# Ranking the expert groups by size and running the smallest group's experts in pairs, in plain fp32 on column strips

## The chip, the cores and the metric

The kernel runs on 1 core of one Trainium2 chip. The metric is the device time of one execution in microseconds (us). TensorE is called PE here (PEld is its weight load), VectorE is DVE, ScalarE is ACT, GpSimd is POOL and SyncE, which issues nearly all DMAs of this kernel, is SP.

## The reference, cut to what matters

Two transformer blocks are computed for 256 tokens of width 1024. The change touches only the last stage, a mixture of 16 experts in four groups of four:

```python
p_group = jax.nn.softmax((t @ w_rg + b_rg).astype(jnp.float32), axis=-1)
g_val, g_idx = lax.top_k(p_group, 1)                 # one group for each token
fine_sel = jnp.take_along_axis(fine, g_idx[:, :, None], axis=1)[:, 0]
e_val, e_idx = lax.top_k(jax.nn.softmax(fine_sel, axis=-1), TOP_K_IN_GROUP)
...
for e in range(N_EXPERTS):
    y_e = (jax.nn.silu(t @ w1[e]) * (t @ w3[e])) @ w2[e]     # 1024x512, 1024x512, 512x1024
    out = out + combine[:, e:e + 1] * y_e
```

Each token belongs to one group, so the four groups' token counts add up to 256, and the smallest group has at most 64 tokens. All weights are fp32: 6 MB for an expert, 96 MB for the stage.

## The kernel before, in words

**Weights.** Every weight is brought by SP in units of 512 KB (128 partitions x 1024 values). A unit lands in a landing buffer (L365, `load_unit`). ACT copies it rounded into a ring of 8 buffers (`weights_hi`, L396, `split_hi`), and DVE subtracts that from the landed unit into a second ring (`weights_lo`, L408, `split_lo`). PE multiplies with both parts in three matmuls (high x high, high x low, low x high: `three`, L443). In the expert stage there are 8 landing buffers (`expert_stage`: four `stage`, two in `x_and_ctx`, two in `work`). SP loads unit u only after `split_lo` of unit u-8 (`lo_ready`), and SP's program is in order: one load that waits holds all behind it. The ring is given back by `unit_used`, which PE raises after a unit's last matmul.

**Experts.** The router's results decide the tokens. The group in the first place is computed densely for all 256 tokens (weights stationary, 8 units "up" for w1 and w3, 4 units "down" for w2). The other three groups have their tokens gathered by selection matrices (`SEL`, 128 slots for each group, matmul L1912) and are computed with the gathered tokens stationary and the weights moving, 512 columns at a time. After four experts of such a group the summed result is split in two parts (`block_hi`, `block_lo`) and scattered back to the tokens by matmuls (`scatter`, L2020). The sequence is written by hand in `SEQ`: dense, four slot experts, dense, four, dense, four, dense.

**Order on the engines.** Step p of the loop does on PE: up with w1, the transposes of the hidden rows of step p-1 (`expert_turn`, L1972), up with w3, and down of step p-1. The units are loaded in the same order: up of p (w1, then w3), then down of p-1. DVE does in step p: the splits of down of p-1 and of up of p+1, with the product of step p (`expert_product`, L3287 and L3294) ahead of the last four splits, and the parts of a scatter in between. ACT does the silu of step p, the hidden rows of p-1 and the 12 splits.

**Set-up.** Between the router and the first expert DVE works out which groups have over 128 tokens, a running sum of those, and from it the slots (L3199 to L3233) and the four first experts for SP (`expert_order`). Then come 8 gathers of 384 columns on PE, each read by two ACT and two DVE instructions (L2449, L2450, L3267, L3270), and the slot weights (L1928).

## Time and profile before

| | us |
|---|---|
| median of 3 runs | 1610.04 |
| lowest, highest | 1608.06, 1612.14 |
| profiled execution: span from the first to the last instruction | 1604.0 |
| what a timed run has beside the span (median less span) | 6.0 |
| PE busy in the span | 1547.5 (96%) |
| expert stage, from PE's first expert matmul at 1257.49 to its last at 1600.04 | 342.6 |

The page gives each engine's busy time. Its strips cut the span into 40 equal slices with a digit each. In the expert stage, the last nine slices, PE stands at 9 throughout, and the DMA strip is at 7 to 9 until the last slice but one. The granted clock is 1.00 in the whole expert stage.

### The profile page before, as it was taken

Reading aid. Unit: us, or ns where it says so; the run is one execution under the profiler, and the core shown is the slowest. Engines: PE = TensorE matmul, PEld = TensorE weight load, DVE = VectorE, ACT = ScalarE, POOL = GpSimd, SP = SyncE. Lnnn points to the kernel's source line nnn. Section 1 sums busy time; section 2 is a strip of 40 time slices with the busy share of each in tenths; the row PEclk is TensorE's granted clock in tenths of the full one; section 3 lists DMA queues with packets and bytes.
Section 4 is the critical chain, followed back from the end, with each engine's and each line's share of the span. In section 5 each row is a group of like instructions: output and inputs, shape, how many; then the busy total and the mean of one; then the engine's idle time right before and its main releaser. Section 6 shows DMA issues by size and latency. Waiting matters only on the chain.

```text
span 1604.0 us, 24065 instructions
## 1 busy us (share of the span) xinstructions
PE 1547.5 (96%) x8757; PEld 1261.9 (79%) x8757; DVE 1090.1 (68%) x1726; ACT 838.2 (52%) x1342; POOL 14.0 (1%) x36
## 2 busy tenths in 40 slices
PE   6999999999999999999999999998998999999999
PEld 3865558988888889888659999886776888889888
DVE  3447764854444446878977676887775687786894
ACT  4326554722322325688864544654453566666672
POOL 2000000000000000000010000000000000000000
PEclk9999999999999999999999999999999999999999
DMA  9588633422332332434525665543220789788792
GB/s 350 162 346 312 247 122 103 153 71 92 103 93 93 103 99 59 122 90 131 173 64 171 192 187 186 171 152 96 93 92 1 263 298 380 247 329 311 256 380 81
DMA packets 195799, 279.69 MB, mean 174 GB/s; under 512 B 12434, under 2 KB 111220, under 8 KB 190588
## 3 DMA queue, kind: packets, MB, share of 16 engines
q1 hardware_dynamic: 194308, 274.21, 50.6%
q0 software_dynamic: 1152, 4.19, 0.7%
q8 instruction: 56, 0.92, 0.2%
q14 instruction: 35, 0.29, 0.1%
q10 hardware_dynamic: 248, 0.09, 0.0%
HBM read 277.40 MB, written 1.05 MB: 174 GB/s over the span
## 4 chain that ended last, share of the span: by engine, by line
PE 76%; DVE 10%; ACT 7%; DMA 3%; issue 2%; SPq 0%; POOL 0%; DVEq 0%; ACTq 0%; POOLq 0%
PE bank L443 66%; DVE weights_lo L408 2%; PE bank L1540 2%; DMA ada_rows_in<-in_ada_w_dram 2%; PE bank L745 1%; ACT weights_hi L396 1%; PE bank L1381 1%; PE bank L1365 1%; DVE work L2781 1%; DVE softmax_cols L2648 1%; PE bank L1349 1%; ACT work L2118 1%; DVE x_and_ctx L590 1%; DMA stage<-in_lru_w_i_dram 1%; DVE work L2639 1%
## 5 line engine op out<-in xcount | busy, mean ns | idle before, releaser
L408 DVE TENSOR_TENSOR weights_lo<-stage,weights_hi 128x1024 fp32r<-128x1024 f32 x324 | 385.1, 1220 | 48.4 <-ACT weights_hi L396 44.6
L396 ACT ACTIVATE weights_hi<-stage 128x1024 fp32r<-128x1024 f32 x324 | 330.1, 1056 | 114.3 <-PE bank L443 69.4
L443 PE MATMUL bank<-act_hi,weights_hi 128*128 128x256 f32 (+1 forms) x1040 | 324.6, 312 | 1.3 <-DVE act_lo L553 1.0
L443 PE MATMUL bank<-act_lo,weights_hi 128*128 128x256 f32 (+1 forms) x1040 | 323.1, 311 | 0.0
L443 PE MATMUL bank<-act_hi,weights_lo 128*128 128x256 f32 (+1 forms) x1040 | 323.1, 311 | 0.0
L443 PE MATMUL bank<-weights_hi,ff_hi 128*128 128x512 f32 x568 | 221.6, 390 | 0.2 <-DVE ff_lo L3031 0.2
L443 PE MATMUL bank<-weights_hi,ff_lo 128*128 128x512 f32 x568 | 221.1, 389 | 0.0
L443 PE MATMUL bank<-weights_lo,ff_hi 128*128 128x512 f32 x568 | 221.0, 389 | 0.0
L443 PEld LDWEIGHTS bank<-act_hi,weights_hi 128*128 128x128 f32 x1040 | 198.3, 191 | 14.5 <-DVE act_lo L553 1.5
L443 PEld LDWEIGHTS bank<-act_lo,weights_hi 128*128 128x128 f32 x1040 | 198.3, 191 | 11.2
L443 PEld LDWEIGHTS bank<-act_hi,weights_lo 128*128 128x128 f32 x1040 | 198.3, 191 | 10.5
L443 PE MATMUL bank<-weights_hi,act_hi 128*128 128x512 f32 (+1 forms) x448 | 177.4, 396 | 6.2 <-ACT work L2315 1.8
L443 PE MATMUL bank<-weights_lo,act_hi 128*128 128x512 f32 (+1 forms) x448 | 173.8, 388 | 0.0
L443 PE MATMUL bank<-weights_hi,act_lo 128*128 128x512 f32 (+1 forms) x448 | 173.5, 387 | 0.0
L845 ACT ACTIVATE turn<-bank 128x512 f32<-128x512 f32 (+1 forms) x48 | 23.6, 492 | 205.6 <-PE bank L443 205.6
L443 PEld LDWEIGHTS bank<-weights_hi,ff_hi 128*128 128x128 f32 x568 | 106.7, 188 | 22.2 <-DVE ff_lo L3031 0.3
L443 PEld LDWEIGHTS bank<-weights_lo,ff_hi 128*128 128x128 f32 x568 | 106.6, 188 | 22.2
L443 PEld LDWEIGHTS bank<-weights_hi,ff_lo 128*128 128x128 f32 x568 | 106.7, 188 | 21.5
L443 PEld LDWEIGHTS bank<-weights_hi,act_hi 128*128 128x128 f32 x448 | 84.6, 189 | 27.8 <-issue 9.2
L867 DVE TENSOR_TENSOR work<-work,bank 128x512 f32<-128x512 f32 x72 | 49.4, 686 | 79.5 <-PE bank L443 79.5
L443 PEld LDWEIGHTS bank<-weights_lo,act_hi 128*128 128x128 f32 x448 | 84.5, 189 | 17.5
L443 PEld LDWEIGHTS bank<-weights_hi,act_lo 128*128 128x128 f32 x448 | 84.6, 189 | 15.6
(404 smaller groups left out, 2018.5 us busy)
## 6 DMA issues: line engine op xcount, KB each, us to landing
stage<-in_mlp_w_dram SPq DMA_DIRECT2D x128, 512.0 KB, 4.0
stage<-in_w_dram SPq DMA_DIRECT2D x96, 512.0 KB, 6.1
ada_rows_in<-in_ada_w_dram SPq DMA_DIRECT2D x40, 1024.0 KB, 6.5
x_and_ctx<-in_w_dram SPq DMA_DIRECT2D x48, 512.0 KB, 5.9
work<-in_w_dram SPq DMA_DIRECT2D x48, 512.0 KB, 6.2
stage<-in_w_in_dram SPq DMA_DIRECT2D x32, 512.0 KB, 4.2
stage<-in_lru_w_in_dram SPq DMA_DIRECT2D x20, 512.0 KB, 3.9
stage<-in_attn_w_qkv_dram SPq DMA_DIRECT2D x12, 512.0 KB, 7.9
```

The source lines that it names most:

```text
L396: act.eng.activation(whi[u % NRING][:], landing(act, u)[:], ACT.Copy).then_inc(sem("hi_ready"), 1)
L408: dve.eng.tensor_tensor(wlo[u % NRING][:], landing(dve, u)[:], whi[u % NRING][:].bitcast(F32), ALU.subtract).then_inc(sem("lo_ready"), 1)
L443: m = pe.eng.matmul(ps, l, r, start=start and j == 0, stop=stop and j == 2, skip_group_check=True)
L590: dve.eng.scalar_tensor_tensor(out=XC[:, tt, :], in0=T, scalar=cc[:, 12 + tt:13 + tt], in1=XC[:, tt, :], op0=ALU.mult, op1=ALU.add).then_i ...
L745: m = pe.eng.matmul(psum[bank][32 * q:32 * q + 32, :], adastat[:, k, :], ada_in[ada_buf(p)][:, q * 512:q * 512 + 512], start=k == 0, stop= ...
L845: act.eng.activation(tbuf[:, m % 2, 0:T], ps[:, 0:T], ACT.Relu).then_inc(*act.free((tag, "h", m)))
L867: dve.eng.tensor_tensor(dst, dst, ps[:], ALU.add).then_inc(*dve.free(key))
L1349: m = t.matmul(ps[:], q, kT[rows, j, :], start=False, stop=True, skip_group_check=True)
L1365: m = t.transpose(ps[:, c0:c0 + P], prob[h % 3][:, i, n * P:(n + 1) * P], ident[:])
L1381: m = t.matmul(ps[64 * a:64 * a + 64, i * P:(i + 1) * P], V[:, kt, 2 * j + i, :], pT[:, n, a, i * P:(i + 1) * P], start=n == 0, stop=n == ...
L1540: t.matmul(psum[2 * n + tt][:], SUM[:, 2 * kp + kk, tt * P:(tt + 1) * P], out_rows(kp, n)[:, kk, :], start=kp + kk == 0, stop=False, skip_ ...
L2118: s.activation(prob[h % 3][:, i, 0:nk], ps[:, 0:nk], ACT.Exp, bias=sm[:, 0, at + i:at + i + 1], scale=HD ** -0.5, accum_out=sm[:, 1, at + ...
```

## The change

Four things change, all in the expert stage and its set-up.

1. DVE ranks the four groups by token count with MAX and MAX_INDEX. The largest group is the dense one, the next two have 128 slots each, and the smallest has 64 slots, held twice side by side. The gather has 320 columns, and of the smallest group only a plain fp32 copy is kept (`GP`).
2. The smallest group's four experts run as two pair steps, one behind the other, between the second and the third dense expert. In a pair step one expert's matmul writes PSUM partitions 0 to 63 and the other's 64 to 127, with 64 stationary columns each (two column strips of the array). Operands are plain fp32, and the moving operand is the landed unit itself: no `split_hi`, no `split_lo`.
3. The units of a pair are not split, so their landing buffers are given back by PE (`unit_used`) instead of by DVE (`lo_ready`).
4. The pair results are added up in a buffer (`YP`) by ACT and DVE (`pair_y`, `pair_add`), split (`pair_hi`, `pair_lo`) and scattered in step 9. The last block of slot experts is scattered in the last down step, as the third block was before.

Steps are numbered by their place in `STEPS` from here on. The units that a text numbers count from the first unit of the expert stage (unit 0) in load order; there are 192 before and after.

```diff
@@ sequence of steps @@
-        SEQ = [0, 4, 5, 6, 7, 1, 8, 9, 10, 11, 2, 12, 13, 14, 15, 3]
+        STEPS = [("dense", 0), ("slots", 4), ("slots", 5), ("slots", 6), ("slots", 7), ("dense", 1), ("pair", 12),
+                 ("pair", 14), ("dense", 2), ("slots", 8), ("slots", 9), ("slots", 10), ("slots", 11), ("dense", 3)]
+        SCATTER_STEP = {6: 0, 9: 2}
@@ load_unit (SP) @@
-                if before >= 0:
-                    sp.eng.wait_ge(sem("lo_ready"), before + 1)
+                if before >= 0 and whole(before):
+                    sp.eng.wait_ge(sem(USED), before + 1)
+                elif before >= 0:
+                    sp.eng.wait_ge(sem("lo_ready"), split_index(before) + 1)
...
@@ expert_up (PE), pair step @@
+                if kind(p) == "pair":
+                    for kq in range(4):
+                        w = pair_begin(pe, (2, 512))
+                        for kk in range(2):
+                            k = 2 * kq + kk
+                            for e in range(2):
+                                mm = t.matmul(ps[HD * e:HD * e + HD, :], GP[:, k, 0:HD], w[e][:, kk, :], start=k == 0,
+                                              stop=k == KT - 1, skip_group_check=True)
+                                if kk:
+                                    mm.then_inc(sem(USED), 1)
...
@@ expert_down (PE), pair step @@
+                    for f in range(4):
+                        w = pair_begin(pe, (1, 1024))
+                        for n in range(2):
+                            for m in range(2):
+                                mm = t.matmul(psum[6 + n][HD * m:HD * m + HD, :],
+                                              HP[:, f, HD * m:HD * m + HD],
+                                              w[m][:, 0, n * 512:n * 512 + 512], start=f == 0, stop=f == 3,
+                                              skip_group_check=True)
+                                if n:
+                                    mm.then_inc(sem(USED), 1)
...
@@ scatter (PE) @@
-                t.wait_ge(*pe.freed(("y", b, n)))
+                t.wait_ge(*pe.freed(("y", b, n)) if b < 2 else pe.at("pair_lo", n + 1))
...
@@ pair results (ACT) @@
+            def pair_y(p):
+                for n in range(2):
+                    at = slice(n * 512, n * 512 + 512)
+                    if p == EXPERT_PAIRS[0]:
+                        s.wait_ge(*act.filled(("yp", p, n)))
+                        s.activation(YP[:, at], plan.bank(("yp", p, n))[:], ACT.Copy).then_inc(*act.free(("yp", p, n)))
+                    else:
+                        s.wait_ge(*act.freed(("yp", p, n)))
+                        s.wait_ge(*act.filled(("sc", 0, n, 1)))
+                        s.activation(Yhl[:, 0, at], YP[:, at], ACT.Copy).then_inc(*act.mark("pair_hi"))
...
@@ loop over the steps (DVE) @@
+            for p in range(LAST + 1):
                 if ends_block(p - 2):
                     block_lo(block_of(p - 2))
+                if p - 2 == EXPERT_PAIRS[1]:
+                    pair_add(p - 2)
...
+                todo = split_count(p - 1, "down") + split_count(p + 1, "up")
                 if p:
                     expert_hidden_lo(p - 1)
-                    split_lo(dve, 2)
-                if ends_block(p - 2):
-                    block_sum(block_of(p - 2), 0)
-                split_lo(dve, 6 if p else 4)
+                    todo = some_lo(todo, 2)
+                if p - 2 == EXPERT_PAIRS[1]:
+                    pair_lo()
+                if p in SCATTER_STEP:
+                    block_sum(SCATTER_STEP[p], 0)
+                todo = some_lo(todo, 6 if p else 4)
                 expert_product(p)
...
+                todo = some_lo(todo, 4)
@@ gather (ACT and DVE), 8 times @@
-                s.activation(G3H[:, d, :], ps[:, TX:384], ACT.Copy, scale=colA[:, d, 0:1]).then_inc(*act.mark("g_hi"))
+                s.activation(GP[:, d, 0:HD], ps[:, TX:320], ACT.Copy, scale=colA[:, d, 0:1]).then_inc(*act.mark("g_hi"))
-                v.scalar_tensor_tensor(out=G3L[:, d, :], in0=ps[:, TX:384], scalar=colA[:, d, 0:1],
-                                       in1=G3H[:, d, :].bitcast(F32), op0=ALU.mult,
-                                       op1=ALU.subtract).then_inc(*dve.free(("gather", d)))
```

**On DVE, from the product that ends the dense or pair work to the scatter's second part.** Before, in the step behind a block of slot experts (the second such place), DVE's rows read as follows; L3287 is the dense product, L3326 the second part of the block's result, L3303 the hidden rows, L408 the split.

```order
L3287 TENSOR_TENSOR work<-work,bank 128x512 [waits bank2_full,bank0_free]
L3287 TENSOR_TENSOR work<-work,bank 128x512 [waits unit_used,bank1_free]
L408 TENSOR_TENSOR weights_lo<-x_and_ctx,weights_hi 128x1024 [waits hi_ready,unit_used] x2
L408 TENSOR_TENSOR weights_lo<-work,weights_hi 128x1024 [waits hi_ready,unit_used] x2
L3326 TENSOR_TENSOR y_hi_lo<-bank,y_hi_lo 128x512 [waits y_hi] x2
L3303 TENSOR_TENSOR ff_lo<-work,ff_hi 128x2x256 [waits e_hi] x2
L408 TENSOR_TENSOR weights_lo<-stage,weights_hi 128x1024 [waits hi_ready,unit_used] x2
L3334 TENSOR_TENSOR x_and_ctx<-x_and_ctx,bank 128x512 [waits bank4_full]
L3334 TENSOR_TENSOR x_and_ctx<-x_and_ctx,bank 128x512 [waits bank5_full]
```

The block's second part (L3326) stands ahead of the splits, and the four splits ahead of it belong to units loaded long before. Now the rows of steps 8 and 9 read so; L447 is the split, L3395 the product of the second pair, L3388 the dense product, L3437 the addition of the pair results, L3444 the second part for the scatter.

```order
L3395 SCALAR_TENSOR_TENSOR turn<-turn,decay_coefs,bank 128x512 [waits unit_used,bank0_free]
L447 TENSOR_TENSOR weights_lo<-stage,weights_hi 128x1024 [waits hi_ready,unit_used] x4
L447 TENSOR_TENSOR weights_lo<-x_and_ctx,weights_hi 128x1024 [waits hi_ready,unit_used] x2
L447 TENSOR_TENSOR weights_lo<-work,weights_hi 128x1024 [waits hi_ready,unit_used] x2
L3388 TENSOR_TENSOR work<-work,bank 128x512 [waits bank2_full,bank0_free]
L3388 TENSOR_TENSOR work<-work,bank 128x512 [waits unit_used,bank1_free]
L3437 TENSOR_TENSOR work<-work,bank 128x512 [waits bank6_free,unit_used]
L3437 TENSOR_TENSOR work<-work,bank 128x512 [waits bank7_free,unit_used]
L3404 TENSOR_TENSOR ff_lo<-work,ff_hi 128x2x256 [waits e_hi] x2
L447 TENSOR_TENSOR weights_lo<-stage,weights_hi 128x1024 [waits hi_ready,unit_used] x2
L3444 TENSOR_TENSOR y_hi_lo<-work,y_hi_lo 128x512 [waits pair_hi] x2
```

All eight splits of the next slot expert's up units (L447, x4, x2, x2) now stand between the second pair's product and the dense product, and two more splits stand ahead of the scatter's second part.

**On SP, the loads of the next slot expert's first units.** Before, at the same kind of place:

```order
L365 ISA [waits lo_ready]
L365 DMA stage<-in_w_2_dram 128x2x512
L365 ISA [waits lo_ready]
L365 DMA stage<-in_w_2_dram 128x2x512
L365 ISA [waits lo_ready]
L365 DMA stage<-in_w_2_dram 128x2x512
L365 ISA [waits lo_ready]
L365 DMA stage<-in_w_2_dram 128x2x512
L365 DMA x_and_ctx<-in_w_2_dram 128x2x512 [waits lo_ready] x2
L365 DMA work<-in_w_2_dram 128x2x512 [waits lo_ready] x2
```

Now, behind the loads of the second pair's w2 (128x1024 rows, for which `lo_ready` is awaited):

```order
L400 ISA [waits unit_used]
L400 DMA stage<-in_w_2_dram 128x2x512
L400 ISA [waits unit_used]
L400 DMA stage<-in_w_2_dram 128x2x512
L400 ISA [waits unit_used]
L400 DMA stage<-in_w_2_dram 128x2x512
L400 ISA [waits unit_used]
L400 DMA stage<-in_w_2_dram 128x2x512
L400 DMA x_and_ctx<-in_w_2_dram 128x2x512 [waits unit_used] x2
L400 DMA work<-in_w_2_dram 128x2x512 [waits unit_used] x2
L400 DMA stage<-in_w_2_dram 128x1024 [waits lo_ready] x4
```

The eight loads of step 9's up units wait for `unit_used`, that is for PE's down step of the second pair, where they waited for a split before.

## Rows read from the trace of the kernel before

**Rows 1.** The page: span, busy time (x instructions), and the DMA strip.
```profile
span 1604.0 us, 24065 instructions
PE 1547.5 (96%) x8757; PEld 1261.9 (79%) x8757; DVE 1090.1 (68%) x1726; ACT 838.2 (52%) x1342; POOL 14.0 (1%) x36
...
DMA  9588633422332332434525665543220789788792
```
**Rows 2.** Busy time by stretch: us, PE, PEld, DVE, ACT, POOL, clock, DMA share, GB/s.
```profile
1345.00:1395.00 50.00, 50.00 (x315) 45.42 (x314) 36.33 (x38) 31.76 (x37) 0.00 (x0) 1.00 0.78 279
```
**Rows 3.** Waits of SP's queue from 1240 to 1604: total us, times, longest.
```profile
SPq L365 <- DVE weights_lo L408: 225.0, 183, 9.1
```
**Rows 4.** PE in order of time: start us, us, engine, line, one slot expert apart.
```profile
1307.84 0.38 PE L1972 MATMUL bank<-ident,turn 128*128 128x128 f32 x2
...
1324.65 0.38 PE L1972 MATMUL bank<-ident,turn 128*128 128x128 f32 x2
```
**Rows 5.** Plain fp32 products: 32- and 64-column strips in time order, full width by group.
```profile
103.52 0.13 PEld L745 LDWEIGHTS bank<-ada_rows_in,ada_stat 128*32 128x32 f32 x4 [0.30 <-issue]
103.95 0.13 PEld L745 LDWEIGHTS bank<-ada_rows_in,ada_stat 128*32 128x32 f32 x4 [0.30 <-issue]
...
124.16 1.97 PE L1381 MATMUL bank<-work 128*64 128x128 f32 x32
...
L1540 PE MATMUL bank<-ada_rows_in,work 128*128 128x512 f32 x64 | 27.7, 593 | 1.2 <-ACT turn L2239 1.2
```
**Rows 6.** Busy time by stretch, columns as in Rows 2, two with DMA full.
```profile
1320.00:1325.00 5.00, 5.00 (x26) 4.13 (x25) 4.55 (x5) 1.57 (x3) 0.00 (x0) 1.00 1.04 420
...
1530.00:1535.00 5.00, 5.00 (x25) 4.14 (x24) 3.21 (x4) 4.27 (x6) 0.00 (x0) 1.00 1.04 394
```
**Rows 7.** DMA issues from 1367.5, behind a pause: the first alone, then four; median us to landing.
```profile
stage<-in_w_dram SPq DMA_DIRECT2D x1, 512.0 KB, 3.6
...
stage<-in_w_dram SPq DMA_DIRECT2D x4, 512.0 KB, 5.1
```
**Rows 8.** ACT in order of time while it waits for landings.
```profile
1336.00 1.06 ACT L396 ACTIVATE weights_hi<-stage 128x1024 fp32r<-128x1024 f32 x1 [0.26 <-DMA stage<-in_w_dram]
1337.31 1.06 ACT L396 ACTIVATE weights_hi<-stage 128x1024 fp32r<-128x1024 f32 x1 [0.25 <-DMA stage<-in_w_dram]
```
**Rows 9.** Groups by line from 1300 to 1600: busy us, mean ns of one.
```profile
L408 DVE TENSOR_TENSOR weights_lo<-stage,weights_hi 128x1024 fp32r<-128x1024 f32 x83 | 96.5, 1219 | 7.6 <-ACT weights_hi L396 7.5
L3303 DVE TENSOR_TENSOR ff_lo<-work,ff_hi 128x512 fp32r<-128x512 f32 x6 | 3.9, 689 | 5.7 <-ACT ff_hi L2480 5.6
L3287 DVE TENSOR_TENSOR work<-work,bank 128x512 f32<-128x512 f32 x6 | 3.8, 680 | 0.0
L396 ACT ACTIVATE weights_hi<-stage 128x1024 fp32r<-128x1024 f32 x82 | 82.3, 1057 | 18.5 <-PE bank L443 14.6 <-DMA stage<-in_w_dram 3.9
L2480 ACT ACTIVATE ff_hi<-work 128x512 fp32r<-128x512 f32 x6 | 3.5, 626 | 2.0 <-DVE work L3287 2.0
```
**Rows 10.** Set-up: DVE in order of time, gather parts by group, PE in order of time.
```profile
1242.45 0.15 DVE L3199 TENSOR_SCALAR work<-bank 128x4 f32<-128x4 f32 x1
...
1245.04 0.75 DVE L3233 TENSOR_SCALAR select<-slot_numbers,work 128x384 fp32r<-128x384 f32 x2
...
L3270 DVE SCALAR_TENSOR_TENSOR gathered_lo<-bank,col_scale,gathered_hi 128x128 fp32r<-128x128 f32 x6 | 2.1, 343 | 0.0
...
1256.16 1.47 PE L1928 MATMUL bank<-work,select 128*128 128x4 f32 x12 [0.20 <-DVE gathered_lo L3270]
1257.49 0.36 PE L443 MATMUL bank<-act_hi,weights_hi 128*128 128x256 f32 x1
```
**Rows 11.** PE behind a pause, and the clock by stretch (columns as in Rows 2).
```profile
1098.52 0.47 PE L443 MATMUL bank<-weights_hi,act_hi 128*128 128x512 f32 x1 [1.83 <-ACT work L2315]
...
1105.68 0.49 PE L1768 MATMUL bank<-ident,work 128*128 128x128 f32 x3
...
1100.00:1102.00 2.00, 2.00 (x6) 1.53 (x5) 1.86 (x5) 0.00 (x0) 0.00 (x0) 0.50 0.83 248
```

More of the change, by code:

```diff
@@ L437, in unit_end, with pair_begin @@
                 plan.entry[key]["full"] = pe.last
+        def pair_begin(pe, shape):
+            views = []
+            for _ in range(2):
+                u = pe.unit
+                pe.eng.wait_ge(*pe.at(*landed(pe, u)))
+                views.append(landing(pe, u)[:].rearrange("p (a b) -> p a b", a=shape[0]))
+                pe.unit += 1
+            return views
         def three(pe, ps, wh, wl, ah, al, start, stop, stationary_weights):
@@ L1953, in expert_up @@
                 ps = pe.take(("h", p, j), 2 * j)
+                if kind(p) == "pair":
[8 more added lines that the diff above has]
+                                    mm.then_inc(sem(USED), 1)
+                    pe.last = (USED, Affine(pe.unit, 0, 1))
+                    plan.entry[("h", p, j)]["full"] = pe.last
+                    return
                 gh, gl, at = slots(block_of(p))
-                if SEQ[p] == 4 and j == 0:
+                if expert(p) == 4 and j == 0:
                     for d in range(KT):
@@ L1976, in expert_down @@
                 c0 = TX * (p % 2)
-                e = SEQ[p]
+                e = expert(p)
+                if kind(p) == "pair":
+                    t.wait_ge(*pe.freed(("T", p)))
+                    for n in range(2):
+                        t.wait_ge(*pe.bank_free(6 + n))
+                        pe.take(("yp", p, n), 6 + n)
+                    for f in range(4):
[8 more added lines that the diff above has]
+                                    mm.then_inc(sem(USED), 1)
+                    pe.last = (USED, Affine(pe.unit, 0, 1))
+                    for n in range(2):
+                        plan.entry[("yp", p, n)]["full"] = pe.last
+                    return
                 for f in range(4):
@@ L2485, in expert_hidden_hi @@
                 ps = plan.bank(("T", p))
+                if kind(p) == "pair":
+                    s.activation(HP, ps[:].rearrange("p (f t) -> p f t", f=4),
+                                 ACT.Copy).then_inc(*act.free(("T", p)))
+                    return
                 s.activation(fhi[:, :, c0:c0 + P], ps[:].rearrange("p (f t) -> p f t", f=4),
@@ L3214, in _ @@
-            for r in range(3):
-                v.tensor_scalar(idx[:, 1 + r:2 + r], upto[:, r:r + 1], 4.0, 4.0 * r, ALU.mult, ALU.add).then_inc(*dve.mark())
-            v.wait_ge(*dve.own())
-            v.tensor_copy(order[:], idx).then_inc(*dve.mark("expert_order"))
-            base = rt(14, 4)
-            v.scalar_tensor_tensor(out=base, in0=wide, scalar=128.0 - 1048576.0, in1=first_slot[:, 0, :], op0=ALU.mult,
+            ranked, slot, one = rt(9, 8), rt(11, 2, 4), rt(13, 4)
+            wide, ahead = rt(10, 4), rt(14, 4, 4)
@@ L3221, in _ @@
+            rank = rt(15, 4)
+            v.wait_ge(sem("slots"), 3)
+            v.scalar_tensor_tensor(out=group_keys[:, 0:4], in0=ps[:, 8:12], scalar=8.0, in1=prio[:], op0=ALU.mult,
                                    op1=ALU.add).then_inc(*dve.mark())
             v.wait_ge(*dve.own())
-            v.scalar_tensor_tensor(out=base, in0=upto, scalar=-128.0, in1=base, op0=ALU.mult, op1=ALU.add).then_inc(*dve.mark())
+            v.max(out=ranked, in_=group_keys[:]).then_inc(*dve.mark())
             v.wait_ge(*dve.own())
-            v.tensor_tensor(slot, ps[:, 0:8].rearrange("p (t g) -> p t g", t=2),
-                            base.unsqueeze(1).to_broadcast([P, 2, 4]), ALU.add).then_inc(*dve.free("count"))
+            v.max_index(out=order[:], in_max=ranked, in_values=group_keys[:]).then_inc(*dve.mark("group_order"))
@@ new lines, in _ @@
+            v.tensor_tensor(ahead, ranked[:, 0:4].unsqueeze(1).to_broadcast([P, 4, 4]),
+                            group_keys[:, 0:4].unsqueeze(2).to_broadcast([P, 4, 4]), ALU.is_gt).then_inc(*dve.mark())
+            v.wait_ge(*dve.own())
+            v.tensor_reduce(rank, ahead, AX.X, ALU.add).then_inc(*dve.mark())
+            v.wait_ge(*dve.own())
+            v.scalar_tensor_tensor(out=slot, in0=rank.unsqueeze(1).to_broadcast([P, 2, 4]), scalar=512.0,
+                                   in1=ps[:, 0:8].rearrange("p (t g) -> p t g", t=2), op0=ALU.mult,
+                                   op1=ALU.add).then_inc(*dve.free("count"))
@@ L3305, in expert_hidden_lo @@
                     return
+                if kind(p) == "pair":
+                    return
                 v.wait_ge(sem("e_hi"), hidden_count(p))
```

219 lines of the change are left out of this document (128 added, 91 removed).

## The prediction, made before the changed kernel was run

> **What bounds the kernel now.** I read the page first: PE is busy for 96% of the span, and the DMA strip stands at 7 to 9 in the expert stage [rows 1]. Then the stage by stretches: in 50 us around two steps PE is busy for all 50 at full clock, and DMA for 0.78 of it [rows 2]. So PE sets the end, with DMA close behind it. The waits of SP's queue come third: loads waited 225 us in all for DVE's splits, 183 times [rows 3]. Landing buffers are full and the stream is held back by consumers, never the other way round. From this the question is what a faster PE finds when it asks for units sooner than now.
>
> **PE work.** Two transposes of the same kind stand one slot expert apart, 16.81 us [rows 4]; four such experts are 67.2. A pair step has 2 x 8 contraction steps up and 4 x 2 down, 24 in all, each of two plain fp32 matmuls of 512 columns, one on each strip. The plain 128x512 product takes 27.7 us for 64 records, 0.43 each, and a plain matmul is two records (L1540 issues 32), so 0.86 [rows 5]. Do two strips share that time? L745's four strips do: each quarter has one record in every 0.43 us. L1381 has strips of 64 columns, in pairs as here: 32 records of 128 columns in 1.97 us, one pair in 0.113 after the last one's 0.27, where 128 columns alone need a quarter of 0.43, that is 0.107 [rows 5]. So a pair step is 24 x 0.86 = 20.6 us, with 0.45 of transposes 21.1, and two are 42.2. PE work falls by 67.2 - 42.2 = 25.0 us. From the other side, strips that don't overlap would make it 83.5 instead, 16 more than now; I take the overlap, which two rows show.
>
> The Trainium skill (TensorE: Matmul & The Clock Gate, "Measured speedup vs the span model") measured 2.38 times for three column strips, a share of 0.79 each. By that rule the two steps' matmuls would be 41.2 / 0.79 = 52 us and the saving 11 less. The rows with four strips at one strip's pace speak against it.
>
> **Set-up.** From the count to the selection DVE does 13 dependent small steps in 2.59 us, 0.2 each [rows 10]; now there are 8, two of them (MAX, MAX_INDEX) not in this trace. At 0.2 each this is 1.0 us sooner; between 0.15 and 0.5 for those two it is 0.4 to 1.1. Then each gather loses DVE's second part, 0.34 long, and the slot weights wait for the fifth gather's DVE part (PE sat idle for it) [rows 10]: five times 0.34 is 1.7, less the overlap of one instruction with the next; I take 1.3. The first expert starts right behind, so 2.3 us sooner; 1 to 3.
>
> **DMA in the pair steps.** With the DMA full, 394 to 420 GB/s were moved [rows 6]; 0.524 MB is 1.25 to 1.33 us a unit, and ACT, waiting for landings, began one each 1.31 [rows 8]. I take 1.32. Behind a pause the first unit landed 3.6 us after its issue, and four issued one behind another had a median of 5.1 [rows 7], where a steady 1.32 would give 3.9; I put the fourth at 9.6 after the first issue. A pair step asks for a unit each 0.86 us, and its whole units sit in the landing buffers till PE has used them.
>
> Count from PE's start of the first pair with eight units landed. Two units are used each 1.72, so the first load goes out at 1.8, the ninth unit lands at 5.4, the twelfth at 11.4, the sixteenth at 16.7, and up ends at 18.4 instead of 14.7 (with the scatter, 0.9). Next come the four w2 units of the dense step: they land at 18 to 22, need ACT 1.06 and DVE 1.22 [rows 9], and the down step needs two of them, since the first block sum, which frees its banks, stands behind two splits on DVE. It starts near 22 and lasts 10.9. In it PE frees no pair unit: eight units of the second pair land by 32.5, then the queue runs dry until 34.8. The next lands at 38.5, the fourth at 44, and the 16 behind it at 1.32 each, the last of the first pair's w2 at 60; the third dense expert's first unit lands at 61.5 and is split at 63.8. PE's own work up to there is 13.8 + 0.9 x 2 + 10.9 + 13.8 + 0.45 + 6.9 = 47.7. Lost: 16 us. If the queue never ran dry and the restarts cost nothing, 37 units by 1.3 still give 56, so 8 is the least; with a landing rate as slow as 1.45 it is 20.
>
> The Trainium skill (DMA: Bandwidth & Descriptors, "Specifications") gives a core about 358 GB/s of HBM. A unit would then be 1.46 us, and this loss near 20. The trace of this core alone shows 394 to 420.
>
> **The step behind the pairs.** The dense expert is 23 us of PE, in which the second pair's eight w2 units land and fill all buffers. The next loads wait for `unit_used` of the down step. Count from its start: first load at 1.8, first landing 5.4, fourth 11.4, eighth 16.7. Down ends at 6.9; the up step's fourth unit is ready at 11.4 + 2.4 = 13.8, so up with w1 ends at 15.1 instead of 12.3: 2.8 lost. Then comes the scatter, and what it waits for stands on DVE behind all of this: eight splits (the last ends at 19.1), the dense product, two parts of 0.68 that overlap a little (20.4), the pair sums, two parts again (21.7), on ACT the second high part (22.2), the silu (22.8) and the hidden rows (23.8), again on DVE their low part (24.5), two splits (26.8), and the first low part of the pairs (27.5) [rows 9]. PE stands from 15.1 to 27.5. Lost in all: 15.2 us; 11 if the splits come as fast as the buffers allow and ACT runs ahead, 18 with landings as late as the worst.
>
> Behind such a pause the clock matters. Behind a wait of 1.83 us on ACT the granted clock was 0.50 for a stretch of 2 us, that is 1.2 of 2.4 GHz, and the 24 matmuls up to the next transposes took 7.2 us. At 0.227 each, (16.81 - 0.45) / 72 of a slot expert [rows 4], they would take 5.4 [rows 11]. I add 1.6 for the one long pause, between 0 and 3.4.
>
> **What costs nothing.** 48 splits fewer on ACT and as many fewer on DVE (1.06 and 1.22 us each [rows 9]) free engines that wait for PE anyway. The pair sums of the first pair (ACT, 2 x 0.6) are under the dense up. The tail is the same as before: scatter, last down, four sums, stores.
>
> **Sum against the profiled execution.** -25.0 - 2.3 + 16 + 15.2 + 1.6 = +5.5. Span 1604.0 + 5.5 = 1609.5; the median has 6.0 more than the span, so 1615.5. Most of PE's saving goes to the two waits.
>
> **The rivals.** What a measurement of this kernel can tell from no change is about 0.3%, or 4.8 us: 1605.2 to 1614.9.
> - No change that can be told: the same mechanisms at the small end, 10 us in the pair steps and 12 behind them: -25 - 2.3 + 10 + 12 + 1 = -4 up to +4.8. For it: both ends above are reachable from rows. Time near 1611. Chance 0.31.
> - Faster: the supply isn't the limit, since PE's stream of whole units and less traffic by ACT and DVE let DMA keep up, and the scatter's operand is ready sooner. 8 in the pairs and 3 behind them: -16, 1594. For it: in the dense steps DMA had pauses to spare (0.78 busy). Against it: no landing can be ahead of a buffer that isn't free, and the DVE order is in the program. Chance 0.12.
> - Slower by strips that don't overlap: from the point where a pair's two matmuls take over 1.3 us, PE rather than the DMA sets the pace. Pairs 83.5, so +16 for PE, no wait in the pairs, 10 behind them, -2.3: +24, 1634. Against it: rows 5. Chance 0.04.
> - Slower by supply: landings at 1.46, or a clock that stays at the lower level while PE waits a third of each step (then a step is 3.4 us and PE-bound): +5 to +10 on the forecast, 1622. Chance 0.06.
> - The forecast, over 1614.9: 0.47.
>
> So slower by over 0.3% has 0.57, no change 0.31, faster 0.12. For eight in ten I leave out the lowest tenth and the upper: 1605 to 1624.
>
> **What would show it.** Right: PE in the two pair steps idle with DMA named as what ended it, DMA share near 1.0 there; one wait of 10 to 14 us at the scatter matmul in step 9, ended by DVE (L3444); PE's busy time about 25 lower; records of the pair matmuls in twos, 0.43 apart; the first expert matmul near 1255. Wrong in the first place: no wait at that scatter, or pair steps of 21 us without waits (then it is faster), or records of the two strips one behind the other (then it is far slower).

## The result, and the profile after

| | before | after |
|---|---|---|
| median of the first comparison, us | 1609.05 (4 runs) | 1625.78 (4 runs) |
| ratio, 95% interval | | 1.0101 (1.0083 to 1.012) |
| median of a second comparison, us | 1609.87 (23 runs) | 1622.91 (6 runs) |
| ratio, 95% interval | | 1.0066 (1.004 to 1.0093) |
| profiled execution, span | 1604.0 | 1621.5 (its own time 1623.24) |

One of the four runs of after (1923.9 at 0.75 of the clock) counts in the median but not in the ratio; without it the median is 1624.75. The change makes the kernel slower, by 0.7 to 1.0%, where 0.3% was forecast (1615.5, with 1605 to 1624 as the range).

The page of after, against [rows 1]: span, PE's busy time, and the strips of the clock and of DMA.

```profile
span 1621.5 us, 23657 instructions
PE 1536.1 (95%) x8653; PEld 1227.2 (76%) x8653; DVE 1032.2 (64%) x1662; ACT 791.2 (49%) x1292; POOL 14.0 (1%) x36
...
PEclk9999999999999999999999999999999999999899
DMA  9588733423233332334435566452221788787692
```

PE's busy time fell by 11.4 us, not by 25. Of the missing 13.6 us 10.5 are work at the lower clock (12.2 us lost in after and 1.7 in before, as counted below); the other 3.1 are not traced. Where the saving went is seen in the expert stage cut at PE's landmarks (columns as in [rows 2]): up to the first pair matmul, the first pair's up, the second dense down, the second pair's up, the first pair's down, the third dense up, the second pair's down, the next slot expert's w1, the wait at the scatter, and what follows.

```profile
1262.30:1386.60 124.30, 124.30 (x738) 110.68 (x737) 87.12 (x86) 72.50 (x82) 0.00 (x0) 1.00 0.81 292
1386.60:1407.30 20.70, 17.10 (x73) 5.76 (x72) 3.35 (x5) 3.96 (x7) 0.00 (x0) 1.00 0.84 315
1407.30:1422.50 15.20, 12.68 (x48) 10.07 (x48) 8.95 (x12) 2.62 (x3) 0.00 (x0) 0.89 0.71 262
1422.50:1440.90 18.40, 15.47 (x69) 4.92 (x68) 1.04 (x2) 1.15 (x2) 0.00 (x0) 1.00 0.85 313
1440.90:1453.00 12.10, 7.75 (x32) 2.29 (x32) 1.23 (x1) 2.11 (x2) 0.00 (x0) 1.00 1.04 397
1453.00:1476.60 23.60, 23.54 (x196) 23.52 (x196) 9.24 (x8) 9.02 (x11) 0.00 (x0) 1.00 0.69 265
1476.60:1485.30 8.70, 7.18 (x34) 2.21 (x32) 1.22 (x1) 2.11 (x2) 0.00 (x0) 1.00 0.57 185
1485.30:1492.70 7.40, 5.93 (x24) 4.32 (x24) 4.90 (x4) 4.23 (x4) 0.00 (x0) 1.00 1.04 396
1492.70:1505.10 12.40, 0.05 (x2) 0.00 (x1) 10.29 (x13) 8.66 (x12) 0.00 (x0) 0.65 0.85 321
1505.10:1514.80 9.70, 9.70 (x33) 7.78 (x34) 7.64 (x8) 3.90 (x4) 0.00 (x0) 0.74 0.71 237
```

Before, every such row reads PE busy for the whole stretch at 1.00. After, the rows without a wait in them are the first (124.3 of 124.3), the third dense up (23.5 of 23.6) and the last (9.7 of 9.7); the 103 us from there to the end have none either. In the rows of the pairs' up PE is idle for 3.6, 2.9 and 4.4 us while DMA moves 313 to 397 GB/s, and one row of 12.4 us has next to no PE at all. What ended PE's waits in the stage, the five largest (total us, times, longest):

```profile
PE bank L2121 <- DVE y_hi_lo L3444: 12.3, 1, 12.3
PE bank L495 <- DVE weights_lo L447: 7.5, 4, 2.5
PE bank L2029 <- DMA work<-in_w_dram: 2.8, 2, 2.1
PE bank L2029 <- DMA stage<-in_w_dram: 2.4, 4, 0.8
PE bank L2069 <- DMA stage<-in_w_dram: 1.9, 2, 1.3
```

And PE in order of time: the pair matmuls (16 records in 3.60 us, two strips in the time of one, as the strips of [rows 5]), a wait for a landing, the dense down, the scatter.

```profile
1390.16 3.60 PE L2029 MATMUL bank<-stage,work 128*64 128x512 f32 x16
...
1398.84 1.94 PE L2029 MATMUL bank<-work 128*64 128x512 f32 x8 [2.08 <-DMA work<-in_w_dram]
...
1409.83 0.47 PE L495 MATMUL bank<-weights_hi,ff_hi 128*128 128x512 f32 x1 [2.53 <-DVE weights_lo L447]
...
1505.10 2.08 PE L2121 MATMUL bank<-y_hi_lo,select_turned 128*128 128x512 f32 x4 [12.35 <-DVE y_hi_lo L3444]
```

For the dense down the profile names the split (L447). What came last there is the first block's sum (L3452), whose first half, 0.69 us long, ends 0.1 us ahead of PE's start at 1409.83:

```profile
1409.05 1.28 DVE L3452 TENSOR_TENSOR x_and_ctx<-x_and_ctx,bank 128x512 f32<-128x512 f32 x2
```

DVE during the long wait shows the order that the prediction read from the program: splits of the next slot expert, dense product (L3388), pair sums (L3437), hidden rows (L3404), two more splits, and at last the scatter's operand (L3444).

```profile
1493.96 2.50 DVE L447 TENSOR_TENSOR weights_lo<-work,weights_hi 128x1024 fp32r<-128x1024 f32 x2
1496.38 1.28 DVE L3388 TENSOR_TENSOR work<-work,bank 128x512 f32<-128x512 f32 x2
1497.57 1.27 DVE L3437 TENSOR_TENSOR work<-work,bank 128x512 f32<-128x512 f32 x2
1500.55 1.29 DVE L3404 TENSOR_TENSOR ff_lo<-work,ff_hi 128x512 fp32r<-128x512 f32 x2 [1.70 <-ACT ff_hi L2576]
1502.08 2.36 DVE L447 TENSOR_TENSOR weights_lo<-stage,weights_hi 128x1024 fp32r<-128x1024 f32 x2 [0.24 <-ACT weights_hi L432]
1504.36 1.28 DVE L3444 TENSOR_TENSOR y_hi_lo<-work,y_hi_lo 128x512 fp32r<-128x512 f32 x2
```

So far the forecast holds. But the first expert matmul is at 1262.34 and was at 1257.49, 4.9 us later instead of 2.3 sooner, though nothing ahead of the set-up was changed. Stretches of after at the granted clock of 0.50 to 0.54 explain it (columns as above):

```profile
124.00:127.00 3.00, 3.00 (x31) 2.98 (x32) 0.66 (x5) 1.54 (x5) 0.00 (x0) 0.54 1.03 429
1257.50:1260.90 3.40, 3.21 (x13) 3.17 (x14) 3.26 (x6) 3.40 (x10) 0.00 (x0) 0.50 1.05 398
1411.10:1414.50 3.40, 3.40 (x10) 2.63 (x9) 3.40 (x5) 0.00 (x0) 0.00 (x0) 0.50 1.05 384
1496.40:1505.10 8.70, 0.00 (x1) 0.00 (x1) 6.76 (x11) 6.53 (x9) 0.00 (x0) 0.50 0.78 285
1505.10:1510.00 4.90, 4.90 (x12) 3.84 (x13) 3.99 (x5) 0.23 (x1) 0.00 (x0) 0.50 0.56 190
```

The first of them stands in code that is the same in both kernels; in before it reads

```profile
124.00:127.00 3.00, 3.00 (x43) 2.72 (x42) 1.44 (x8) 1.79 (x6) 0.00 (x0) 1.00 1.03 429
```

with 12 matmuls more in the same 3 us. A stretch at 0.50 costs half of PE's busy time in it. Counted so over the whole trace, before lost 1.7 us to the clock, all at 1099.6, and after 12.2: 6.5 ahead of the set-up (of it 3.1 and 1.7 in two stretches at 1100 and 1134 that are not shown), 1.6 in it, 4.2 in the expert stage. So of the 17.5 us between the two spans 10.5 are the clock's.

### The profile page after: what moved, and what is told of

Read it like the earlier page. It is cut to its first block, busy times and chain, and to the rows that moved or that the text cites. A ratio compares the mean times of both kernels' runs of the same rounds, so it can differ in the third digit from the quotient of the medians.

```text
span 1621.5 us, 23657 instructions
## 1 busy us (share of the span) xinstructions
PE 1536.1 (95%) x8653; PEld 1227.2 (76%) x8653; DVE 1032.2 (64%) x1662; ACT 791.2 (49%) x1292; POOL 14.0 (1%) x36
## 4 chain that ended last, share of the span: by engine, by line
PE 70%; DVE 13%; ACT 7%; DMA 6%; issue 3%; SPq 1%; POOL 0%; DVEq 0%; ACTq 0%; POOLq 0%
PE bank L495 59%; DVE weights_lo L447 3%; DMA stage<-in_w_dram 2%; PE bank L1609 2%; ACT weights_hi L432 2%; DMA ada_rows_in<-in_ada_w_dram 2%; PE bank L797 1%; PE bank L1450 1%; PE bank L1434 1%; DVE work L2892 1%; PE bank L2029 1%; DVE x_and_ctx L2892 1%; DVE softmax_cols L2759 1%; PE bank L1418 1%; ACT work L2214 1%
## 5 line engine op out<-in xcount | busy, mean ns | idle before, releaser
L447 DVE TENSOR_TENSOR weights_lo<-stage,weights_hi 128x1024 fp32r<-128x1024 f32 x300 | 358.0, 1221 | 103.2 <-ACT weights_hi L432 96.7
L432 ACT ACTIVATE weights_hi<-stage 128x1024 fp32r<-128x1024 f32 x300 | 306.3, 1055 | 148.7 <-PE bank L495 67.7
L495 PE MATMUL bank<-weights_hi,ff_hi 128*128 128x512 f32 x536 | 210.6, 393 | 2.6 <-DVE weights_lo L447 2.5
L495 PE MATMUL bank<-weights_lo,ff_hi 128*128 128x512 f32 x536 | 209.8, 391 | 0.0
L495 PE MATMUL bank<-weights_hi,ff_lo 128*128 128x512 f32 x536 | 209.7, 391 | 0.0
L897 ACT ACTIVATE turn<-bank 128x512 f32<-128x512 f32 (+1 forms) x48 | 23.6, 491 | 206.4 <-PE bank L495 206.4
L495 PEld LDWEIGHTS bank<-weights_hi,ff_hi 128*128 128x128 f32 x536 | 101.4, 189 | 24.0 <-DVE weights_lo L447 2.9
L495 PEld LDWEIGHTS bank<-weights_lo,ff_hi 128*128 128x128 f32 x536 | 101.2, 189 | 21.4
L495 PEld LDWEIGHTS bank<-weights_hi,ff_lo 128*128 128x128 f32 x536 | 101.5, 189 | 20.5
L495 PEld LDWEIGHTS bank<-weights_hi,act_hi 128*128 128x128 f32 x448 | 85.4, 191 | 33.0 <-issue 12.3
```

Source lines behind the costliest of these rows:

```text
L432: act.eng.activation(whi[r % NRING][:], landing(act, u)[:], ACT.Copy).then_inc(sem("hi_ready"), 1)
L447: dve.eng.tensor_tensor(wlo[r % NRING][:], landing(dve, u)[:], whi[r % NRING][:].bitcast(F32), ALU.subtract).then_inc(sem("lo_ready"), 1)
L495: m = pe.eng.matmul(ps, l, r, start=start and j == 0, stop=stop and j == 2, skip_group_check=True)
L897: act.eng.activation(tbuf[:, m % 2, 0:T], ps[:, 0:T], ACT.Relu).then_inc(*act.free((tag, "h", m)))
```

## The experiments

For each profile three numbers serve below: the stage (first to last expert matmul), what the clock cost in it, counted as above, and the difference of the two. The timed runs were made in six comparisons, each with its own runs of before, whose median lay between 1608.6 and 1610.5; across comparisons the ratios to before are the safer measure. "Both" is the kernel with both reorderings of DVE that are described below, and "fillers" are matmuls that PE computes in its waits and nobody reads.

| kernel | median, us | ratio to before, 95% | stage | clock in stage | stage less clock |
|---|---|---|---|---|---|
| before (first profile) | | | 342.5 | 0 | 342.5 |
| before again | 1608.93 | 0.9993 (0.9979 to 1.0007) | 342.5 | 0 | 342.5 |
| after (first profile) | 1625.78 | 1.0101 (1.0083 to 1.012) | 355.1 | 4.2 | 350.9 |
| after again | 1622.91 | 1.0066 (1.004 to 1.0093) | 358.6 | 9.4 | 349.2 |
| sum first | 1622.57 | 1.007 (1.0048 to 1.0091) | 352.1 | 2.2 | 349.9 |
| pair results early | 1609.96 | 0.9995 (0.9978 to 1.0012) | 340.6 | 3.4 | 337.2 |
| both | 1606.58 | 0.9974 (0.9957 to 0.999) | 338.6 | 4.7 | 333.9 |
| quarter loads | 1611.47 (one run) | | 342.7 | 4.7 | 338.0 |
| pairs apart | 1609.89 | 0.9989 (0.997 to 1.0008) | 342.2 | 2.9 | 339.3 |
| down early | 1606.82 | 0.998 (0.9964 to 0.9995) | 338.2 | 0 | 338.2 |
| down early, fillers | 1603.68 | 0.996 (0.9947 to 0.9972) | 340.9 | 1.7 | 339.2 |
| after, fillers | 1614.34 | 1.0031 (1.002 to 1.0042) | 351.6 | 1.7 | 349.9 |
| both, fillers | 1602.10 | 0.9955 (0.9938 to 0.9972) | 335.5 | 0 | 335.5 |
| before, fillers | 1608.06 | 0.9987 (0.9973 to 1.0) | 342.5 | 0 | 342.5 |

**The two kernels again, unchanged.**

> The kernel before, unchanged. Its first profile shows one dip of the granted clock to 0.5 (3.4 us long, 1.7 us lost) in the whole span, the changed kernel's shows five ahead of the pair steps' own. Theory 'chance': the dips ahead of the expert stage come and go from one execution to the next in both kernels; then this profile has another number of them (2 to 5, span 1606 to 1611) at other places than 1100, and its timed runs spread in steps of about 1.7 us. Rival 'program': the kernel before has one dip ahead of the stage in each execution; then the profile again reads 1604 with a mean clock of 0.999.

> The changed kernel, unchanged. Theory 'chance': the dips at 124, 1134 and 1257 us of its first profile are not there again, or others are; PE's first expert matmul, 1262.3 in the first profile, moves by the dips' cost alone, 1.7 us each; the dips behind the waits of 2.5 and 12.3 us in the stage return or not, the waits themselves return within 0.5 us. Rival 'program': the same dips at the same places, first expert matmul again at 1262.3.

The profile of before now has a span of 1608.5. The stretch near 1100 is there again (at 1101.3, moved by the 1.7 us that one at 1077 cost), and two places are new, 1077 and 1193, where two are joined:

```profile
1077.40:1080.80 3.40, 3.40 (x8) 1.93 (x8) 3.30 (x6) 1.08 (x1) 0.00 (x0) 0.50 0.35 86
1101.30:1104.70 3.40, 3.40 (x10) 2.63 (x9) 3.19 (x7) 0.00 (x0) 0.00 (x0) 0.50 0.76 207
1193.40:1200.30 6.90, 5.95 (x14) 4.78 (x15) 3.95 (x6) 2.97 (x5) 0.00 (x0) 0.51 0.36 109
```

They cost 6.4 us, and its stage is 342.5 as before: the extra 4.5 us lie ahead of it. Over the 107 timed runs of before behind the first comparison the mean clock was 0.999 in three, and 0.992 to 0.998 in the others: the profile that I forecast from was one of the rare good ones. After again has its stretch at 124 no more, but others, among them 13.6 us around the start of the stage:

```profile
1256.20:1269.80 13.60, 12.40 (x57) 11.95 (x56) 12.17 (x17) 11.95 (x22) 0.00 (x0) 0.50 1.04 385
1501.90:1515.60 13.70, 6.10 (x14) 4.79 (x15) 10.21 (x14) 7.59 (x10) 0.00 (x0) 0.50 0.71 240
```

'Chance' is right for which stretches come ahead of the set-up, but not for where: every one of the 14 profiles has one near 1077 or near 1100, in before as in the changed kernels, and several places return. Nor is it the whole: one near 1257 (1251 to 1258) is there in all eight profiles of changed kernels without fillers (below), and in neither of the two of before; and one of 13.7 us, which starts inside the 12.3 us wait and goes on behind it, is there in all four profiles that have the wait unfilled. The wait itself came back at 12.3 both times. First expert matmul less the clock's cost ahead of it: 1255.8 and 1255.6 before, 1254.3 and 1254.0 after. The set-up is 1.6 us shorter.

Why the stretch near 1257 came with the change stays open. PE pauses there for 2.29 and 1.28 us in after, and the kernel before has nearly the same pauses at the same two gathers, with the clock at 1.00 in both of its profiles:

```profile
1250.98 0.44 PE L1912 MATMUL bank<-select,xn_hi 128*128 128x384 f32 x1 [2.10 <-DVE gathered_lo L3270]
...
1253.63 0.45 PE L1912 MATMUL bank<-select,xn_hi 128*128 128x384 f32 x1 [0.97 <-DVE gathered_lo L3270]
```

**Pair results early.** In DVE's loop (the dense product moves up together with the pair results and leaves its old place behind the splits; ACT takes the high part of the pair results behind the first two of its splits):

```diff
-                if p - 2 == EXPERT_PAIRS[1]:
-                    pair_add(p - 2)
...
+                if p - 1 == EXPERT_PAIRS[1]:
+                    expert_product(p)
+                    pair_add(p - 1)
                 if p:
                     expert_hidden_lo(p - 1)
                     todo = some_lo(todo, 2)
-                if p - 2 == EXPERT_PAIRS[1]:
+                if p - 1 == EXPERT_PAIRS[1]:
                     pair_lo()
...
-                expert_product(p)
+                if p - 1 != EXPERT_PAIRS[1]:
+                    expert_product(p)
```

> The changed kernel, where DVE takes in step 8 the dense product, the addition of the pair results and their low part ahead of the last six splits of the next slot expert, and ACT the high part behind the first two. Nothing else changes. Theory 'DVE's order' (my forecast's step behind the pairs): the wait of 12.3 us at the scatter goes, and with it the clock's 2.5 us; PE then waits for up w3's units only by their landings (1.3 us each against 1.36 that PE needs): 12 to 15 us faster than the changed kernel, about 1612. Rival 'supply': the units behind the restart at 1478 are late anyway, so the wait comes back in up w3 and in the dense down (whose hidden rows stand behind the splits on ACT): at most 6 us faster, about 1620.

13 us faster than after, in the same comparison: 'DVE's order'. The wait at the scatter is gone, and 12.0 of the 13 us are in the stage less clock. The pair sums (L3441) and their low part (L3448) now stand between splits that wait for landings anyway, five microseconds ahead of the scatter at 1493.60:

```profile
1483.86 1.28 DVE L3441 TENSOR_TENSOR work<-work,bank 128x512 f32<-128x512 f32 x2 [6.30 <-PE bank L2069]
1485.06 2.35 DVE L447 TENSOR_TENSOR weights_lo<-stage,weights_hi 128x1024 fp32r<-128x1024 f32 x2
1487.34 1.28 DVE L3448 TENSOR_TENSOR y_hi_lo<-work,y_hi_lo 128x512 fp32r<-128x512 f32 x2
```

**The first block's sum ahead of two splits.**

```diff
+                if p in SCATTER_STEP and SCATTER_STEP[p] == 0:
+                    block_sum(SCATTER_STEP[p], 0)
                 if p:
                     expert_hidden_lo(p - 1)
                     todo = some_lo(todo, 2)
...
-                if p in SCATTER_STEP:
+                if p in SCATTER_STEP and SCATTER_STEP[p]:
                     block_sum(SCATTER_STEP[p], 0)
```

> The changed kernel, where DVE takes the first block's sum (which frees the two banks that the dense down step waits for) ahead of the two splits in step 6. Theory 'bank': down starts 2 us sooner, the clock dip behind the 2.5 us wait (1.7 us) goes in most executions, and since the landings behind wait for PE they start sooner too: 2 to 4 us faster, about 1622.5. Rival 'supply': the stretch is bounded by landings at 1.33 us each from 1389 to 1470, where PE's start of down doesn't matter: under 1 us.

> Both reorderings of DVE in one kernel: the dense product and the pair results ahead of the last splits, and the first block's sum ahead of the splits in step 6. Theory 'supply': the second adds 0 to 1 us, since in the pair steps landings at 1.33 us each set the pace: time as with the first alone, 1609 to 1610. Theory 'bank': 2 to 4 us better, 1606.5.

The wait ahead of the dense down fell from 2.53 to 0.59 us, yet the median is only 0.3 us lower, within the interval, and the stage less clock is that of after: 'supply'. Together with the first reordering the median is 3.4 lower than with that one alone and the stage less clock 3.3, but the two were timed in different comparisons and their intervals overlap (0.9978 to 1.0012, 0.9957 to 0.999). In the two profiles PE's idle time in the stage is 15.7 and 12.5 us. Whether it gives 3 us there stays open. The pair of them is faster than before, by 0.3%.

**A quarter of each pair load.**

```diff
                 dst = dst.rearrange("p (a b) -> p a b", a=dims[0])
+                if late(sp, u) and whole(u):
+                    q = dims[1] // 4
+                    dst, src = dst[:, :, 0:q], src[:, :, 0:q]
```

> The changed kernel, where each load of the two pair steps brings a quarter of its columns; the rest of the moving operand is whatever the buffer held, so the output is not the reference's. Theory 'supply' (the landings bound the pair steps): of the 16 waits between 1386 and 1453 that end with a landing nearly all go, the stretch from the first pair matmul to the next dense up falls from 66.4 to about 50 us (47.7 of work, 2.5 for the bank), the 12.3 us wait at the scatter stays, since it hangs on loads behind the pairs. Rival 'restart' (the waits come from loads that are issued late, whatever their size): the stretch stays above 60 us.

The kernel leaves out three quarters of each of these loads, so its output is not the reference's. From the first pair matmul to the next dense up it takes 52.4 us instead of 66.4, and no wait there ends with a landing any more:

```profile
1389.80:1442.20 52.40, 49.12 (x221) 21.87 (x221) 14.76 (x19) 9.84 (x13) 0.00 (x0) 1.00 0.49 151
```

The same loads were issued at the same events, so it is their size: 'supply'. PE's own work in the stretch is 49.1, where I had 47.7.

**Pairs apart, and a pair's down step early.**

```diff
-                 ("pair", 14), ("dense", 2), ("slots", 8)
+                 ("dense", 2), ("pair", 14), ("slots", 8)
```

> As the kernel with both reorderings, but the sequence is dense, four slots, dense, pair, dense, pair, four slots, dense: the pair steps have the third dense expert between them; the pair results are scattered in step 10. Theory 'supply': a pair step needs 24 units (31.7 us at 1.32) in 21 us of PE, 10.7 more than it has, and eight landed buffers cover most of that; a dense expert behind it (34 us for 12 units, 15.8 us of DMA) fills them again. PE's idle time in the stage falls from 15.7 us (pair results early) to 4 to 8, with fewer clock dips: 1600 to 1603, faster than the kernel before by 0.4 to 0.6%. Rival 'restart': each pair step still ends with a dry queue, and the loads behind it wait for PE's down step; the idle time only moves: 1607 to 1610.

Not faster than with the pairs in a row: PE's idle time is 16.7 us against 12.5. The second pair now starts with a wait ahead of every quarter of w1, since the first pair's eight w2 units hold all landing buffers through a dense up. So the next kernel turned a pair's hidden rows and took its down step in the middle of the next step's up with w1.

```diff
+            def between(p, j, kq):
+                if j == 0 and kind(p - 1) == "pair":
+                    if kq == down_at(p) // 2:
+                        expert_turn(p - 1)
+                    if kq == down_at(p):
+                        expert_down(p - 1)
```

> As the kernel with the pair steps apart, but a pair's hidden rows are turned in the middle of the next step's up with w1, and its down step follows there: behind two of four quarters of a dense up, behind all four of a slot up. The pair's eight w2 units, which fill all landing buffers, are so given back 17 us sooner (dense behind the pair) and 5 us sooner (slots behind it). SP, ACT and DVE keep the same order of units. Theory 'buffers held' (a dry queue behind each pair is what is left): the second pair finds eight landed units, PE's waits in the stage fall from 16.7 to 5 to 9 us, the wait of 2.6 us ahead of the slots' up goes or falls under 1.5: 8 to 12 us faster than with the pairs apart, 1598 to 1602, faster than the kernel before by 0.5 to 0.7%. Rival 'demand': a pair step takes units faster than they land whatever stands ready, so waits come back within its w1: at most 3 us, 1607.

3 us better in the median and 1.1 in the stage less clock, so the rival 'demand' was right. The second pair does find its first eight units, and then waits from its second half on; and the slot expert behind it, which asks for a unit each 1.36 us, waits for the splits of a stream that is still starting:

```profile
1452.00 1.94 PE L2051 MATMUL bank<-stage,work 128*64 128x512 f32 x8 [0.60 <-DMA stage<-in_w_dram]
1454.75 1.94 PE L2051 MATMUL bank<-stage,work 128*64 128x512 f32 x8 [0.82 <-DMA stage<-in_w_dram]
...
1489.23 0.47 PE L503 MATMUL bank<-weights_hi,act_hi 128*128 128x512 f32 x1 [1.22 <-DVE weights_lo L455]
1493.38 0.50 PE L503 MATMUL bank<-weights_hi,act_hi 128*128 128x512 f32 x1 [1.15 <-DVE weights_lo L455]
1498.56 0.47 PE L503 MATMUL bank<-weights_hi,act_hi 128*128 128x512 f32 x1 [2.13 <-DVE weights_lo L455]
```

The waits moved, and most of them stayed.

**PE kept busy in its waits.** The fillers are plain bf16 matmuls of 0.22 us into unused banks, in four kernels; `keep_busy` is a helper that both kernels already use elsewhere (79 records in the trace of before). The places in after:

```diff
+                if d in (4, 6):
+                    keep_busy(pe, 3, 10 if d == 4 else 5)
                 if plan.uses[4 + d % 4]:
                     t.wait_ge(*pe.bank_free(4 + d % 4))
                 ps = pe.take(("gather", d), 4 + d % 4)
...
+                if p == 5:
+                    keep_busy(pe, 6, 10)
...
             def scatter(b, n):
+                if b == 2 and n == 0:
+                    keep_busy(pe, 1, 52)
```

> The changed kernel, with PE kept busy by bf16 matmuls of 0.22 us into unused banks where it waited: 10 and 5 ahead of the fifth and seventh gather, 10 ahead of the dense down step in step 6 (the wait of 2.5 us), 52 ahead of the scatter in step 9 (the wait of 12.3 us). The waits themselves stay. Theory 'clock' (the part of the measured excess that my forecast lacked is the granted clock behind pauses): no dips at these four places, the stage falls to its length less dips, about 350, and the time by 5 to 9 us, to 1614 to 1618. Rival 'places only': the dips come elsewhere instead and the time stays within 2 us of the changed kernel's, 1621 to 1625.

The median is 8.6 us below that of after again (1614.34 against 1622.91), in another comparison. Over before it is 5.7 us (1.002 to 1.0042) where after had 13.0 (1.004 to 1.0093, which just touches it) and 16.7 (1.0083 to 1.012). The stage less clock is 349.9, as in after (350.9 and 349.2): the waits are where they were. The long wait is filled, and the matmuls behind it run at full clock:

```profile
1485.80:1498.20 12.40, 11.39 (x53) 5.00 (x52) 10.23 (x13) 8.71 (x12) 0.00 (x0) 1.00 0.83 316
1498.20:1505.00 6.80, 6.74 (x30) 5.58 (x31) 6.55 (x9) 3.26 (x4) 0.00 (x0) 1.00 0.72 231
```

This is close to the 5.5 of my sum, but in part by luck. Without the clock the sum had 3.9, and the profiles show 6.7: the span less the clock's cost is 1609.0 here and 1602.3 in the first profile of before. The fillers also left this kernel a better mean clock than before had in the same comparison (0.998 against 0.996).

> The same, with 10 and 5 matmuls of bf16 into an unused bank on PE ahead of the fifth and seventh gather, where it waited 2.3 and 1.3 us. Theory 'pauses': the dips of the granted clock near 1257 (in all seven profiles of the changed kernel and its variants, in none of the two of before; 1.5 to 6 us lost) come from these pauses: they go, and the time falls by 1.5 to 4 us. Rival 'chance': a dip there as often as before, and the fillers (3.2 us of work in 3.6 us of waiting) change nothing or cost up to 0.5 us.

> The kernel with both reorderings of DVE (pairs in a row, 1606.6), with the 10 and 5 fillers ahead of the fifth and seventh gather alone. Theory 'clock': its dips near 1255 (5.1 us of dip in its profile, 3 us lost in the set-up and more in the first dense step) go: 1602 to 1604, faster than the kernel before by 0.4%. Rival 'chance': 1606 to 1607.

> The kernel before with the same 10 and 5 fillers ahead of its fifth and seventh gather. Theory 'its set-up has no dip to lose' (both profiles of it show none there): within 1 us of the kernel before, 1608 to 1610, so what the fillers gave to the changed kernels (4.5 us) belongs to a cost that the change had brought in. Rival 'the fillers help any version': 2 to 4 us faster than the kernel before, 1605 to 1607; then the best version's lead over the kernel before is that much smaller when both have them.

The set-up's fillers gave 3.1 us with a pair's down step early (1606.82 to 1603.68, in one comparison) and 4.5 us with both reorderings (1606.58 to 1602.10, across two). In both cases the intervals of the ratios to before overlap, but no profile with the fillers has a stretch of half clock in the set-up, and each one of a changed kernel without them has. In before they gave 0.13% (0 to 0.27%), about 2 us: between the two theories and not settled, since neither of its profiles without them has anything to win there. So the two rivals, a cost that the change brought in and a gain that any version would have, share what the set-up's fillers gave. Both reorderings with the fillers are the best version: 1602.10, 0.45% faster than before (0.28 to 0.62). Of that lead 0.13% may be the fillers' alone, by what they gave to before.

## Why the prediction was wrong, point by point

- **PE work, -25.** Right in kind: the strips overlap. The size was a little off. The stretch that quarter loads left free of waits for landings took 49.1 us of PE, not 47.7.
- **Set-up, -2.3.** Right, 1.6 less once the clock is taken out. But a stretch of half clock came with the change: 1.6 and 3.2 us in the set-up of the two profiles of after.
- **DMA in the pair steps, +16.** The stretch from the first pair matmul to the third dense up was 66.4 where I had 63.7. Of the 2.7, 1.7 is a stretch at half clock (1411). The other 1.0 is PE's own work (49.1, by quarter loads, against 47.7), less 0.4 in the waits. Nearly all landings came 1.27 to 1.37 us apart, against 1.32 in the forecast. The rival of a slower supply would have needed 1.46.
- **The step behind the pairs, +15.2.** From its start to the scatter 28.4 us, forecast 27.5; the wait 12.3, forecast 12.4; named engine and line as forecast.
- **The clock, +1.6: this is the step that failed.** I priced one pause, and took the rest of the kernel's clock from a profile that had lost 1.7 us in all. Behind that pause the clock cost 2.5 and 3.1 us in the two profiles of after, where I had 1.6: the row that I priced it from shows 2 us of a stretch of 3.4, and here it lasted 13.7, with PE busy in the last 4.9 and 6.1 of them. In the whole stage it cost 4.2 and 9.4 us, in the set-up 1.6 and 3.2. Each of the waits that I had forecast can bring such a stretch behind it; I put it behind one. Of the 17.5 us between the first two spans 10.5 are the clock's, where the sum had 1.6, and the other 7.0 stand against 3.9. Of the 10.5, 4.8 lie in code that did not change, ahead of the set-up, and say nothing of the change. With fillers in the waits the kernel came from 13.0 and 16.7 us over before to 5.7, at the same stage less clock; up to 2 us of that may be what fillers give to any version. Two of my signs failed by the clock too: the first expert matmul came at 1262.3 instead of near 1255, and PE's busy time fell by 11.4 instead of 25. The Trainium skill (TensorE: Matmul & The Clock Gate, "A second HAM failure mode: psum-queue depth-cycling") says that short idle times between groups of matmuls can be frequent enough to make the clock swing. The traces agree for the set-up of after, with pauses of 2.29 and 1.28 us and 0.50 at 1257.5; they do not for that of before, where pauses of 2.10 and 0.97 us left the clock at 1.00.
- **The baseline.** The 6.0 us beside the span were in truth 1.7 (1623.24 less 1621.5, and 1.7 to 2.0 in every run) and some 4.3 us of clock that the profiled execution had been spared. Since I carried the 6.0 over whole, this did not shift the forecast; but it hid that the clock was a cost with a size of its own, and one that a change with new pauses makes larger.

## What to carry to other kernels

When a change puts pauses into a stage in which PE had none, price the clock behind every pause, not behind the longest, and look at more than one profile of the kernel before for what the clock costs it already. An operand that one engine prepares for another should stand in its program where its inputs are ready, not behind work that waits for transfers: here that order, with the dense product moved along, was 13 us. Cheaper arithmetic on units that must still come from memory moves the bound to the transfers: of PE's 25 us, 7 to 9 were left in the stage less clock of the best orders, and neither spreading the steps nor giving buffers back sooner won more.

## What the runs showed of the hardware

- The granted clock fell to 0.50 for 3.4 us or several times that, mostly behind pauses of PE of 0.8 to 2.6 us, but also at 124.2, with no pause over 0.5 us in the 10 us ahead of it: there in one execution of after and not in another.
- Behind such pauses the lower clock came in some executions and not in others. In the wait of 12.3 us it came in all four profiles that had it unfilled, 2.2 to 4.7 us after PE went idle. Bf16 matmuls of 0.22 us in place of the pause kept it at 1.00.
- Two column strips of 64 in plain fp32, 512 columns each: 16 records in 3.60 us, which is one strip's pace (0.43 us a record).
- Behind a dry queue the first unit landed 3.7 to 4.4 us after its issue (four restarts of after). In two of the three in the pair steps and behind them one later gap was 3.1 to 3.4 us; else nearly all units came 1.27 to 1.37 us apart.
